# Clearing the semaphores of a stage by ranges of numbers, in a two-layer hybrid-attention trunk on one core

## The reference

```python
def even_layer(x, mem, ...):
    h = rmsnorm(x, norm_g)
    qa, ka, va, ga, qb, kb, vb, gb, qm, gm = split_cols(h @ w_in, EVEN_SPLITS)
    oa = sliding_window_sink_attention(qa, ka, va, sinks)      # 8 heads, window 128
    ob = stick_breaking_attention(qb, kb, vb)                  # 8 heads, strictly causal
    om = memory_attention(qm, rmsnorm(mem, mem_norm_g), w_mem_kv)
    y = concatenate([oa * silu(ga), ob * silu(gb), om * silu(gm)])
    return x + y @ w_out

def odd_layer(x, mem, ...):
    h = rmsnorm(x, norm_g)
    qc, ckv, qi, ki, wi, gc, qm, gm = split_cols(h @ w_in, ODD_SPLITS)
    oc = dsa_sparse_attention(qc, rmsnorm(ckv), w_uk, w_uv, qi, ki, wi)   # top 256 keys of each query
    om = memory_attention(qm, rmsnorm(mem, mem_norm_g), w_mem_kv)
    y = concatenate([oc * silu(gc), om * silu(gm)])
    return x + y @ w_out
```

## Time and profile before

| | us |
|---|---|
| median of 3 runs | 3970.88 |
| lowest and highest of them | 3966.53, 3973.17 |
| the profiled execution's own time | 3967.44 |
| its span | 3965.6 |
| mean granted clock of TensorE, share of full speed | 0.96 |

### The profile page before, as it was taken

How to read it: one execution, slowest core, us unless ns; L and a number is a source line. 1 busy time by engine, 2 the same in 40 slices (tenths; PEclk the granted TensorE clock), 3 DMA queues, 4 the chain that set the end, 5 groups by cost and what they waited for, 6 DMA issues and landing times. The chain is left out here.

```text
span 3965.6 us, 83573 instructions
## 1 busy us (share of the span) xinstructions
PE 3577.3 (90%) x32524; PEld 3080.1 (78%) x32524; DVE 2307.9 (58%) x5832; ACT 2063.7 (52%) x4636; POOL 766.7 (19%) x657
## 2 busy tenths in 40 slices
PE   5999999888899989978779989965799999999899
PEld 4777999877687768857658988954688888888687
DVE  6100110066899973320799989976577777777322
ACT  4222111156788862212677657643577777777311
POOL 3222100012566640002005325223100000000000
PEclk9999999999899989989899999988899999999899
DMA  5332321283643223452313354245544433341432
GB/s 191 111 117 106 125 78 46 66 208 97 136 97 75 67 80 130 149 189 101 85 43 134 110 168 141 79 151 197 137 95 98 97 86 89 87 98 45 147 121 79
DMA packets 330574, 441.64 MB, mean 111 GB/s; under 512 B 18376, under 2 KB 253000, under 8 KB 319944
## 3 DMA queue, kind: packets, MB, share of 16 engines
q1 hardware_dynamic: 248024, 318.55, 30.0%
q10 hardware_dynamic: 82176, 117.98, 8.0%
HBM read 272.37 MB, written 164.10 MB: 110 GB/s over the span
## 5 line engine op out<-in xcount | busy, mean ns | idle before, releaser
L1245 PEld LDWEIGHTS s_o<-s_v,s_pT 128*64 128x64 f32 x13056 | 401.8, 138 | 87.5 <-issue 67.3
L1245 PE MATMUL s_o<-s_v,s_pT 128*64 128x64 f32 x13056 | 436.2, 224 | 18.5 <-issue 18.5
L211 PE MATMUL s_acc<-s_wh,s_hT 128*128 128x256 f32 (+1 forms) x1408 | 430.0, 305 | 7.1 <-ACT s_parts L624 3.1
L1411 ACT ACTIVATE s_probs<-s_probs,s_nmx 128x512 f32<-128x512 f32 (+3 forms) x640 | 417.0, 657 | 29.2 <-DVE s_nmx L1457 29.2
L212 PE MATMUL s_acc<-s_wl,s_hT 128*128 128x256 f32 (+1 forms) x1408 | 428.9, 305 | 0.0
L213 PE MATMUL s_acc<-s_wh,s_hT 128*128 128x256 f32 (+1 forms) x1408 | 428.6, 304 | 0.0
L1230 PE MATMUL s_s<-s_kh,s_qs 128*128 128x512 f32 (+3 forms) x944 | 377.9, 403 | 50.3 <-DMA s_kl<-kc 24.4
L211 PE MATMUL s_acc<-s_hT,s_wh 128*128 128x512 f32 x880 | 350.7, 399 | 67.7 <-DVE s_wl L310 30.0
L1446 DVE CUSTOM_DVE_ANT_0 s_probs<-s_s,s_scores 128x512 f32<-128x512 f32 (+3 forms) x640 | 371.7, 607 | 25.5 <-issue 25.3
L2196 DVE TENSOR_SCALAR_CACHE_REDUCE s_scratch<-s_scores,s_thr 128x384 uint8<-128x384 f32 (+4 forms) x320 | 365.3, 1209 | 1.1
L212 PE MATMUL s_acc<-s_hT,s_wh 128*128 128x512 f32 x880 | 347.4, 395 | 0.0
(11 more groups left out here) (248 smaller groups left out, 7731.2 us busy)
## 6 DMA issues: line engine op xcount, KB each, us to landing
fm<-s_parts ACTq DMA_DIRECT2D x120, 512.0 KB, 2.8
s_qs<-fm SPq DMA_DIRECT2D x60, 512.0 KB, 6.5
y<-s_g SPq DMA_DIRECT2D x20, 1024.0 KB, 5.1
s_y<-y SPq DMA_DIRECT2D x32, 640.0 KB, 6.0
s_q<-fm SPq DMA_DIRECT2D x64, 256.0 KB, 9.9
kc<-s_parts ACTq DMA_DIRECT2D x32, 512.0 KB, 2.9
s_kh<-kc SPq DMA_DIRECT2D x30, 512.0 KB, 11.3
s_kl<-kc SPq DMA_DIRECT2D x30, 512.0 KB, 12.9
```

The source lines that it names most:

```text
L211: nc.tensor.matmul(out, sh, mh, start=(j == 0), stop=False)
L1245: last = nc.tensor.matmul(o_ps[r:r + HD, 0:HD], pT[:, x * P + r:x * P + r + HD], v[:, g.u.kbs[g.a + x], vc:vc + HD], start=(g.first and x ...
L1411: nc.scalar.activation(e, e, ACT.Exp, bias=nmx[:, us:us + 1], scale=slope[2 * u.j + u.hh], accum_out=rsum[:, us, part:part + 1]).then_inc( ...
```

## The change

In the clearing block the numbers of the scope's semaphores are sorted and gone through once; for each run of consecutive numbers one clear instruction over the whole run is issued. Which semaphores are cleared, by which engine, and in which block stays as it was.

```diff
             with self.nc.Block() as block:
                 @block.sync
                 def _(sp):
-                    for s in self.taken:
-                        sp.sem_clear(s)
+                    numbers = sorted(s.num for s in self.taken)
+                    first = numbers[0]
+                    for n, after in zip(numbers, numbers[1:] + [None]):
+                        if after != n + 1:
+                            sp.sem_clear(range(first, n + 1))
+                            first = after
         self.ctx.close()
```

## The result

The changed kernel took 3947.88 us, the median of 6 runs (3942.04 to 3953.95), against 3967.81 us for the kernel before in 6 runs (3961.05 to 3973.17). The ratio is 0.9949, with a 95% interval of [0.9938, 0.9959]: 16 to 25 us less. It is faster by 0.5%, beyond the 0.2% that can be told from no change. The forecast was 3955 us with a range down to 3948, so the time lies 0.1 us outside it.

The account below looks back on a forecast made before the run. TensorE's matmuls bound most stages, but SP's clears alone set the clearing blocks. Clears 15.3 + longer steps 0.8 - block floor 0.3 = 15.8 us less; 3970.88 - 15.8 = 3955.1, predicted 3955, range 3948 to 3963 (8 in 10).

Parts of the forecast that it names:

- The price of a clear and its cover: Stage ends: each clear on SP costs 55 ns, nothing covers it; 279 steps go, 15.3 us.
- The sum of the clearing blocks: All 15 blocks between stages: 15.8 us less, leaving about 2.5 us.
- The long steps of 0.7 us: Three clearing blocks with steps over 55 ns; with 0.4 us before a drain, 0.8 us taken as won, bounds 0 and 1.1.
- What a clear of a range costs: Clearing blocks: a range costs what one clear does, 55 ns whatever its length.
- the flat price: Clearing blocks: 55 ns per range clear regardless of how many numbers it holds.
- The walk rival: Clearing blocks: a range is walked at 25 ns a number, so only 8.4 us won, 3962.5 us; chance 0.07.
- The estimate of 29 ns a number: Program-end reset of 51 semaphores in about 1.5 us; by that price 301 numbers would still cost about 8.7 us.
- The hidden fetch: Stage starts: clears cover fetching the next stage's code; 10.8 of 15.8 us given back, 3965.9 us; chance 0.08.
- The later clock: Stage starts: TensorE's clock rises later; 31.6 us more at 0.50 cancels the gain; chance 0.03, to slower than before.
- What moves: SP's list: shorter by 279, code pieces end elsewhere, stalls 0.3 to 0.5 us; taken as 0, 1 us either side.
- the upper bound of 16.9 us: Whole program: top of the forecast's own gain range, 15.0 to 16.9 us by its bounds.

Follow-up runs that it names:

- the doubled clears: Kernel before with every clear issued twice, 602 clears; 3984.07 us, ratio 1.0040.
- the halves: Changed kernel with the old count of clears back in only the first seven scopes, or only the last eight: 3958.12 us, ratio 0.9984; 3961.62 us, ratio 0.9983.

## Why the prediction was right or wrong

*The price of a clear and its cover.* Right. 55 ns a step: the old count put back took the gain away, and the same clears under a wait of SP cost nothing. The prediction leans here also on clears up to 1460.6 us, which stand in no row; this is the row:

```profile
L95 SPq EVENT_SEMAPHORE_RANGE_CLEAR  x19: 25/25/25, 1459.7 to 1460.6; - x19
```

*The sum of the clearing blocks.* Forecast 15.8 us less, measured 15.4. From the first clear to GpSimd's last report the 15 blocks sum to 18.3 us before and 2.9 after, where the prediction had about 2.5. The long steps of 0.7 us and the 0.4 us ahead of the drain went with the clears, slightly more than the 0.8 I took. What made the gain smaller all the same are the records of the ranges: the 22 together are 0.5 us longer than 22 of 25 ns. With a range of 36 SP's drain ends 0.13 us after the start of the clear and not at 0.07, so SP and not TensorE is again the last to report in the ends with long ranges.

*What a clear of a range costs.* I took the flat price; 31 to 90 ns were measured, nearly flat. The record does grow with the numbers, but by 1.6 ns for each and not by 25. The walk rival is refuted.

The estimate of 29 ns a number, which I had worked out from the Trainium skill's page "Runtime: NRT & Kernel Launch", section "The ~15µs preamble/postamble breakdown", does not hold for a range inside the program: this case's rows give 90 ns for 37 numbers, 2.4 ns each. What that reset itself takes, no run here shows.

*The hidden fetch.* Refuted. Two first loads were late before, the one of project that the prediction saw (0.95 us behind SP's leaving of the meeting, 0.47 now) and the one of sparse attention, which is not in the earlier trace rows (0.39, and 0.07 now). Where nothing was late, nothing became so.

*The later clock.* Refuted. Outside the standstills the time at the lower clock did not grow: it is 1 us less, good to 3 us, and the rival needed 31.6 us more.

*What failed: the size of the whole, in the step "What moves", where I took 0 with 1 us on either side.* In the pooled runs the stages took 3.4 us less, with an interval of about 2 us around it. The step had the right kind of event in it, a stall that hangs on the place in SP's list, but counted it at nothing, although the 0.9 us at the start of project stood in the earlier trace rows: 0.8 us of it went at two stage starts. No experiment gave the rest a mechanism. Beside it, the three runs that I started from had a median of 3970.9 us where 106 runs have a mean of 3968.7. So the forecast of 3955.1 becomes, by the pooled means, 3955.1 - 2.2 (start) + 0.4 (clearing blocks) - 3.4 (stages) = 3949.9 us. That this is the measured mean of 3949.8 proves nothing, since the 3.4 us are what was left over. The six runs shown first lay another 1.9 us lower, at 3947.9, and this set them 0.1 us outside the range. The range allowed for scatter about the forecast, but not for the starting median's own and for an unforeseen term at the same time; with three runs that spread over 6.6 us, it should have reached 3 us lower. Its sum also has a slip: the upper bound of 16.9 us does not come out of the terms, which give 15.3 + 1.1 - 0.3 = 16.1, or 17.1 with the 1 us of "What moves". That the time fell just outside the range and not just inside is luck: the other three times the changed kernel's median was 3949.0 to 3951.8 us, inside it.

What stays open: whether what is left of the 3.4 us, some 2 us, is a cost of standstills that are spread over the stage starts, further waits that hang on the place of an instruction, or chance in a set of runs that scatter by 4 to 5 us each. The table's rows differ, the doubled clears do not fit them, the halves do not decide, and one of four comparisons shows no such gain at all.

## What to carry to other kernels

Where four engines wait in a meeting for the fifth, every instruction of the fifth counts in full, however short its record is: price it by the distance between two starts (here 55 ns for a record of 25 ns, and 59 for one of 17 ns), not by its duration, and look for it in the rows of the sequencer, since the busy shares leave it out. Then ask whether it must stand there at all: 279 clears put under a wait cost nothing. A gain of this kind is found by the length of the blocks in two traces, here to 0.03 us, long before the total times can show it; and a stage that differs by 5 us in two pairs of traces may still be scatter, so take a further trace of the same program before explaining it. Where runs from several chips are pooled, look also at each beside its own baseline: the baselines here lie 4 us apart, as much as the effect that was sought.

## What the runs showed of the hardware

A clear of consecutive semaphore numbers by SP records about 28 ns and 1.6 ns for each number (31 ns for 2, 40 for 10, 66 for 26, 90 for 37). Clearing one semaphore again and again is slower than clearing ever another one: 60 ns a step in the middle with 30 ns recorded, against 55 with 25; raising one takes 59 with 17.

How late SP's first load comes behind a meeting went with the number of instructions in SP's list before it, whatever these cost: 0.95 us behind the meeting with 77 ahead of it in six traces, 0.47 us with 40, 117 or 319 in ten; and 0.38 us with 778 in four, 0.07 us with other numbers in twelve.
